# Output weights brought in and split during the last attention pass, half of the first output tile computed there, and that pass unrolled in another order

## The reference, cut to what matters

```python
s = jnp.einsum('bqhnd,bkhnd->bnhqk', q, k) * (1.0 / math.sqrt(HEAD_DIM))   # n = 0, 1: two score maps
a = jax.nn.softmax(s, axis=-1)
a = a[:, 0] - lam * a[:, 1]
attn = jnp.einsum('bhqk,bkhv->bqhv', a, v)
...
mix = jnp.concatenate([pool, attn], axis=-1) @ w_out
x = x + gate1 * mix
h2 = rms_norm(x, norm2_g) * (1 + scale2) + shift2
aff = softmax(h2 @ w_router)
```

## Time and profile before

| what | value |
|---|---|
| median of 3 runs | 3293.43 us (3290.72 to 3294.23) |
| the profiled execution | 3294.67 us, of it 3293.0 us from the first to the last instruction |
| PE busy with products | 3132.0 us (95%) |
| PE busy with weight loads | 2953.8 us (90%) |
| DVE, ACT, POOL busy | 2258.2 us (69%), 1640.5 us (50%), 650.2 us (20%) |
| mean granted clock of PE | 0.981 |

### The profile page before, as it was taken

One profiled execution on the slowest core, in us unless ns is written; L12 is line 12 of the kernel. 1 busy time (PEld: TensorE's weight loads), 2 busy tenths in 40 slices (PEclk: granted clock), 3 DMA queues, 4 the chain that ended last, 5 costly groups with the idle time before them and its releaser, 6 DMA issues. The chain is left out here.

```text
span 3293.0 us, 69969 instructions
## 1 busy us (share of the span) xinstructions
PE 3132.0 (95%) x23550; PEld 2953.8 (90%) x23550; DVE 2258.2 (69%) x3849; ACT 1640.5 (50%) x3632; POOL 650.2 (20%) x862
## 2 busy tenths in 40 slices
PE   6999999999999999998979985999999999999998
PEld 4988989989989999997768874999999999999998
DVE  4888888878878888878874447555555555555553
ACT  4556666666656656665652114443443444444442
POOL 2532333333333333331000001000100000000001
PEclk8999999999999999999989997999999999999999
DMA  8654344444344344433326544666666666665663
GB/s 286 239 196 131 120 146 125 127 130 137 118 134 141 121 128 153 127 101 102 112 96 245 192 156 141 192 188 189 199 187 188 190 188 186 189 192 180 191 187 97
DMA packets 373848, 530.69 MB, mean 161 GB/s; under 512 B 29658, under 2 KB 321754, under 8 KB 358490
## 3 DMA queue, kind: packets, MB, share of 16 engines
q1 hardware_dynamic: 363996, 494.52, 46.2%
q0 software_dynamic: 9728, 34.61, 4.6%
HBM read 439.10 MB, written 89.16 MB: 160 GB/s over the span
## 5 line engine op out<-in xcount | busy, mean ns | idle before, releaser
L2610 PE MATMUL ps_gu<-xT,e_w 128*128 128x272 f32 x6144 | 786.2, 290 | 2.1 <-DVE xT L2794 2.1
L2610 PEld LDWEIGHTS ps_gu<-xT,e_w 128*128 128x128 f32 x6144 | 776.8, 188 | 2.5 <-issue 2.3
L2783 DVE TENSOR_TENSOR e_w<-e_raw,e_w 128x2048 fp32r<-128x2048 f32 x190 | 435.3, 2291 | 413.6 <-ACT e_w L2683 413.6
L1082 ACT ACTIVATE e<-ps_s,negm 128x1024 f32<-128x1024 f32 (+2 forms) x416 | 474.3, 1146 | 257.2 <-DVE negm L1472 200.5
L1457 DVE TENSOR_REDUCE mx<-ps_s 128x1 f32<-128x1024 f32 (+3 forms) x428 | 524.4, 1233 | 78.5 <-PE ps_s L745 77.8
L745 PE MATMUL ps_s<-kT,qT 128*128 128x512 f32 (+1 forms) x1920 | 472.7, 385 | 12.6 <-ACT e L1082 11.6
L745 PEld LDWEIGHTS ps_s<-kT,qT 128*128 128x128 f32 x1920 | 341.9, 190 | 88.7 <-ACT e L1082 31.1
L2629 PE MATMUL ps_gu<-hid,e_w 128*128 128x272 f32 x3072 | 412.2, 291 | 0.0
L819 PE MATMUL ps_m<-w,hT 128*128 128x384 f32 x2040 | 391.7, 340 | 3.9 <-DVE o L1524 3.9
L2629 PEld LDWEIGHTS ps_gu<-hid,e_w 128*128 128x128 f32 x3072 | 392.2, 188 | 0.0
L787 PE MATMUL ps_m<-v,aT 128*128 128x128 f32 x2816 | 370.8, 277 | 1.2 <-ACT aT L1068 1.2
(11 more groups left out here) (333 smaller groups left out, 3472.8 us busy)
## 6 DMA issues: line engine op xcount, KB each, us to landing
hT<-hT_d SPq DMA_DIRECT2D x85, 1024.0 KB, 5.3
e_raw<-w_gate SPq DMA_DIRECT2D x64, 1024.0 KB, 5.0
e_raw<-w_up SPq DMA_DIRECT2D x64, 1024.0 KB, 5.0
e_raw<-w_down SPq DMA_DIRECT2D x64, 1024.0 KB, 5.6
tab<-tabs_d SPq DMA_DIRECT2D x85, 256.0 KB, 2.7
hT_d<-hT SPq DMA_DIRECT2D x17, 1024.0 KB, 3.9
cat_o<-cat_d SPq DMA_DIRECT2D x17, 1024.0 KB, 6.0
w_lent<-w_ada SPq DMA_DIRECT2D x16, 1024.0 KB, 5.5
```

The source lines that it names most:

```text
L1082: nc.scalar.activation(out, src, ACT.Exp, bias=negm[:, s.par, c:c + 1], scale=HD ** -0.5, accum_out=acc).then_inc(exp_done.sem, 1)
L2610: mm = nc.tensor.matmul(ps_gu[:, 2 * (s % 2) + f, 0:SLOTS], w_view(s, a)[:, k, f * P:f * P + P], xT[:, b, k, :], start=(k == 0 and a + b = ...
L2783: nc.vector.tensor_tensor(w[:, s % RING, 1, :], raw[:, s % RAW, :], w[:, s % RING, 0, :].bitcast(F32), ALU.subtract).then_inc(w_lo, 1)
```

## The change

Seven edits. (1) Pass 6 is written out, 17 steps without a loop. (2) SP loads w_out's eight blocks in step 2 of pass 6, into SBUF of that stage that pass 6 no longer uses. In steps 4 to 11 ACT rounds one block at the end of its step, and POOL subtracts it in four pieces of 128x256. (3) At the end of step 15 SP loads `cat` of tile 0, and `last_body` of PE computes k = 0 to 3 of tile 0's products between its steps. (4) `stage_output` keeps w_out and that `cat` where they are, starts tile 0 at k = 4, and loads and splits no w_out. (5) The modulation's result moves from `ps_m` to the fifth bank of `ps_s`: it waits for the maxima of c0 instead of for evacuate, `weighted` 0 no longer waits for its copy, and in that bank exp c0 g2 waits for it and scores c1 g2 for its copy. (6) PE, ACT and DVE get another order in late steps. (7) `last_body` begins with `turn` 4 of p. The late step then reads:

```diff
+SPLIT_FROM, LOWS, KS_AHEAD = 4, 4, 4
 def run_steps(eng, h, body):
+    if h == H:
+        for i in range(NT):
+            body(Slot(h, i))
+        return
...
+        def split_of(s):
+            return s.i - SPLIT_FROM if s.h == H and SPLIT_FROM <= s.i < SPLIT_FROM + KD else None
+        def mod_at(s):
+            return ps_s[:, KEYS + P:KEYS + P + 64] if late(s) else ps_m[:, 0:64]
...
+            def load_out(s):
+                qkv_ready.wait(sp, s)
+                s_ready.wait(sp, s)
+                for k in range(KD):
+                    sp.dma_start(wo_raw[k], io["w_out"][0, k * P:k * P + P, :]).then_inc(side_in, 16)
+            def load_first_rows(s):
+                first = Slot(H, 1)
+                sp.wait_ge(side_in, 16 + 16 * KD)
+                cat_saved[first.par].wait(sp, first, 16)
+                cat_saved[1 - first.par].wait(sp, first)
...
+                pv_part.wait(sp, s)
+                sp.dma_start(g.cat_first.bitcast(F32).rearrange("p k l n -> p (k l n)"),
+                             g.cat[0].rearrange("p k l c -> p (k l c)")).then_inc(side_in, 16)
             def body(s):
+                if s.h == H and s.i == 2:
+                    load_out(s)
+                if s.h == H and s.i == NS - 1:
+                    load_first_rows(s)
...
+                    if n == 2 and c == 1:
+                        mod2_done.wait(pe, s, 1)
...
-                    mod2_done.wait(pe, s, 1 if late(s) and (s.j is not None or s.i < NS) else 0)
+                    mod2_done.wait(pe, s)
...
-                o_done.wait(pe, s, 0 if late(s) else 1)
+                if late(s):
+                    mx_part.wait(pe, s, maxima_of(s))
+                else:
+                    o_done.wait(pe, s, 1)
...
+            def first_rows(k):
+                for a, b in ((0, 0), (0, 1), (1, 0)):
+                    for half in range(2):
+                        nc.tensor.matmul(ps_s[:, 512 * half:512 * half + 512], g.cat_first[:, k, a, :],
+                                         g.wo[b][k][:, 512 * half:512 * half + 512], start=(k == 0 and a + b == 0), stop=False)
             def last_body(s):
                 p = previous(s)
+                turn(p, 4)
                 weighted(p, 3)
                 weighted(p, 4)
+                pe.wait_ge(side_in, 16 + 16 * KD + 16)
+                pe.wait_ge(side_hi, 1 + KD)
+                pe.wait_ge(side_lo, 1 + LOWS * KD)
+                exp_done.wait(pe, s)
+                first_rows(0)
                 turn(s, 0)
+                first_rows(1)
                 weighted(s, 0)
                 turn_out(p)
+                first_rows(2)
                 o_lo.wait(pe, s)
+                first_rows(3)
                 turn_out(s)
...
 # ScalarE, GpSimd
+                    if n == 2 and c == 0:
+                        ada2_done.wait(act, s, 1)
...
+                if split_of(s) is not None:
+                    k = split_of(s)
+                    act.wait_ge(side_in, 16 + 16 * KD)
+                    nc.scalar.copy(g.wo[0][k], wo_raw[k]).then_inc(side_hi, 1)
...
+                if split_of(s) is not None:
+                    k = split_of(s)
+                    pool.wait_ge(side_hi, 1 + k + 1)
+                    for n in range(LOWS):
+                        sl = slice(D // LOWS * n, D // LOWS * (n + 1))
+                        nc.gpsimd.tensor_tensor(g.wo[1][k][:, sl], wo_raw[k][:, sl],
+                                                g.wo[0][k][:, sl].bitcast(F32), ALU.subtract).then_inc(side_lo, 1)
...
 # stage_output
-            for k in range(KD):
-                sp.dma_start(w_raw[:, k, :], io["w_out"][0, k * P:k * P + P, :]).then_inc(wraw_in[k], 16)
-                if k == 0:
-                    load_cat(0, 0)
+            sp.sem_inc(cat_in[0], 16)
+            load_cat(1, 1)
             load_row(0, 0, gate_in)
             load_x(0, 0, 0)
-            load_cat(1, 1)
...
-                for k in range(KD):
-                    if isinstance(t, int) and t == 0:
-                        pe.wait_ge(whi, k + 1)
-                        pe.wait_ge(wlo, k + 1)
+                for k in range(KS_AHEAD if isinstance(t, int) and t == 0 else 0, KD):
```

More of the change, by code:

```diff
@@ L698, in _, with scores @@
         def _(pe):
-            def scores(s, c):
+            def scores(s, c, some=slice(None)):
                 head = s.h - 1
-                if c == 0:
+                if c == 0 and not some.start:
                     if s.front == "sample":
@@ L712, in scores @@
                             v_copied.wait(pe, s)
-                for n, (lo, hi) in enumerate(groups_of(s)):
+                for n, (lo, hi) in list(enumerate(groups_of(s)))[some]:
+                    if n == 2 and c == 1:
+                        mod2_done.wait(pe, s, 1)
                     if c == 1 and s.front == "sample":
@@ L975, in late_body @@
                 p = previous(s)
-                scores(s, 0)
+                scores(s, 0, slice(0, 1))
+                if late(p):
+                    turn(p, 4)
+                scores(s, 0, slice(1, None))
                 if late(p):
@@ L987, in late_body @@
                 weighted(s, 1)
-                turn(s, 3)
+                weighted(s, 2)
                 if late(p):
@@ L1705, in late_body @@
                 mix(s, 2)
-                mix(s, 3)
                 for n in range(len(groups_of(s))):
@@ L1713, in late_body @@
                     normal_out(p)
+                mix(s, 3)
                 mix(s, 4)
@@ L1860, in sem, with fill_to @@
             return sems[-1]
-        w_raw = sb("wo_raw", [P, KD, D])
-        w = sb("wo", [P, 2, KD, D], F32R)
-        rows = sb("mod_rows", [P, 2, 3, D])
-        g2 = sb("g2", [P, D])
-        cat = sb("cat_o", [P, 2, KD, 2, P], F32R)
+        def fill_to(name, address):
+            start = aligned(nc.sbuf_base)
+            assert start <= address
+            if start < address:
+                sb(name, [P, (address - start) // 4])
+            assert aligned(nc.sbuf_base) == address
+        fill_to("wo_in_kT", g.home["kT"] + 4 * 2 * KEYS)
         xt = sb("x_o", [P, 2, D])
         x1 = sb("x1", [P, 2, D])
+        g2 = sb("g2", [P, D])
+        fill_to("free_kT", g.home["v"])
+        sb("cat_first", [P, KD * 2 * P])
         h2 = sb("h2", [P, 2, D])
+        fill_to("wo_in_raw", g.home["w"])
+        rows = sb("mod_rows", [P, 2, 3, D])
+        fill_to("wo_in_w", g.home["hT"] + 4 * 4 * KD * P)
+        cat = [g.cat_first, sb("cat_second", [P, KD, 2, P], F32R)[:]]
         h2T = sb("h2T", [P, KD, P])
@@ L1883, in stage_output @@
         ps_l = ctx.enter_context(nc.psum_tensor("ps_l", [P, 512], F32))
-        wraw_in, whi, wlo = [sem(f"wo_in{k}") for k in range(KD)], sem("wo_hi"), sem("wo_lo")
         gate_in, rows_in, rows_made = sem("gate_in"), sem("rows_in"), sem("rows_made")
@@ L2053, in body @@
                     sl = slice(512 * half, 512 * half + 512)
-                    nc.vector.tensor_tensor(x1[:, par, sl], ps_y[:, par, half, :], rows[:, prompt, 0, sl],
+                    nc.vector.tensor_tensor(x1[:, par, sl], y_of(t, par)[:, half, :], rows[:, prompt, 0, sl],
                                             ALU.mult).then_inc(gated, 1)
@@ L2078, in _ @@
         def _(act):
-            for k in range(KD):
-                act.wait_ge(wraw_in[k], 16)
-                nc.scalar.copy(w[:, 0, k, :], w_raw[:, k, :]).then_inc(whi, 1)
             def exponentials(t):
```

78 lines of the change are left out of this document (54 added, 24 removed).

## The result

| | before | changed |
|---|---|---|
| median of the runs (range), us | 3293.83 (3290.72 to 3297.70), 4 runs | 3273.16 (3270.16 to 3274.29), 4 runs |
| profiled execution, its span, us | 3294.67, 3293.0 | 3274.29, 3272.6 |
| instructions | 69,969 | 69,178 |

The ratio is 0.9938 (95% interval 0.9923 to 0.9953): the changed kernel is 20.7 us faster, by the interval some 15 to 25. Run again beside others it took 3275.52 (3271.41 to 3276.23, 5 runs), ratio 0.9935 (0.9922 to 0.9949).

A forecast was written before the change was run, and what follows sets the result against it. It took PE and DVE as nearly full in late steps, transfers as binding the output stage's front, and PE after it. Terms of -15.9, +0.5, +1.6, +0.7, +0.8 and -14.1 sum to -26.4: 3293.4 becomes 3267.0 us, range 3257 to 3282.

The forecast's parts named there:

- Term 2: POOL's subtractions in pass 6: 32 pieces delay DVE by 0.2 us in each of 8 steps, +1.6 us.
- Term 3: Pass 6's end: step 16 costs +0.7 us and the products added to last_body +0.8 us.
- Term 4: Output stage's front: with w_out already loaded, rows land earlier and tile 2 starts at 1739.5 instead of 1753.59, -14.1 us.
- Term 1: Pass 6's late steps: the new order and unrolling cut the period from 13.28 to 12.15 us, -15.9 us over 14 steps.
- DVE's floor: Late step of pass 6: DVE's own sequence without its waits for scores, 11.95 us, the least for any order.
- Rival A: Late steps: lateness goes round in the new order, period stays at 13.0 us, total 3279 us; chance 0.17.
- Rival C: Late steps: POOL's pieces block DVE's mixes, +10 to +22 us, total 3277 to 3289; chance 0.07.
- Rival D: Unrolled pass 6 starves for instructions: a gap in each of 12 steps, +40 us, total 3307; chance 0.04.
- Step 1: Step 1 of pass 6: moving mix 3 behind `negm` puts up to 0.7 us on the path, +0.5 us.
- Step 16: Pass 6's end: evacuate of tiles 14 and 15 each comes 0.35 us later behind turn 4, +0.7 us.
- last_body: Pass 6's end: of the added blocks of tile 0's products, the second delays the prompt's weighted, +0.8 us.
- Rival B: Output stage's front: tile 0's chain is late by itself, gain only 6 us, total 3275 us; chance 0.10.

The follow-up runs named there:

- experiment 1: The kernel before with pass 6 written out and nothing else: 3296.15 us, ratio 1.0003 to the kernel before.
- experiment 2: The changed kernel with the old order of late steps and the modulation back in `ps_m`: 3286.64 us, ratio 0.9971 to the kernel before.
- experiment 7: The changed kernel with the low halves of w_out subtracted by DVE, one 128x1024 in each of eight steps, none by POOL: 3279.50 us, ratio 0.9951.
- experiment 6: The changed kernel without products of tile 0 computed ahead in `last_body`; w_out still loaded early: 3276.66 us, ratio 0.9946.
- experiment 5: The changed kernel with, in step 1 alone, `turn` 0 and 1 ahead of the modulation and mix 3 ahead of c1's maxima: 3272.26 us, ratio 0.9930.
- experiment 8: The changed kernel with the edits of experiments 3, 4 and 5 together: 3265.68 us, ratio 0.9912 to the kernel before.
- experiment 10: The kernel of experiment 8 run again, side by side with the changed kernel: 3264.81 us, ratio 0.9906 to the kernel before.
- experiment 3: The changed kernel with, in step 16 alone, turn 4 and weighted 3 ahead of the prompt's scores: 3270.26 us, ratio 0.9927.
- experiment 9: The changed kernel itself run again, side by side with the kernel of experiment 10: 3275.52 us, ratio 0.9935 to the kernel before.
- experiment 4: The changed kernel with `cat` of tile 2 issued ahead of tile 0's stores instead of behind its store of h: 3267.71 us, ratio 0.9914.

## Why the prediction was right, and where it was off

The time, 3273.16, is in the range of 3257 to 3282 and 6.2 us above the 3267.0 forecast, near the upper end of the forecast's own range (3259 to 3274). The forecast's likeliest case is what happened, 20.7 gained instead of 26.4. Part of how near it came is luck: Term 2 was put 1.6 too high and so made up for some of what Terms 3 and 4 lacked, and 2.0 of the 20.4 us between the two traces lie ahead of all that was edited.

**Term 1 holds.** 12.17 against the 12.15 taken, 13.16 outside the loop before. That it is the order and the bank, and not the unrolling or the early load, experiments 1 and 2 show: with the pass written out alone, and with the early load, POOL's pieces and the half tile on top of that, the period stays at 13.16. It is 0.22 above the 11.95 that the prediction called DVE's floor, and experiment 7 shows that DVE bounds it. The wait that is left stands where the layout put it, ahead of the second maximum of c1, but also ahead of that of c0, where it looked for none. Rival A (the order closes on itself) falls with the period.

**Term 2 was an overestimate: 0 instead of +1.6.** Steps with pieces (1579.50 to 1591.66, 12.16) and the mean of all 14 (12.17) are the same; `on` takes 0.28. The pieces lie where the layout put them, 2.7 us ahead of N to N + 0.1. Rival C falls: 32 pieces of 0.73 beside DVE's maxima cost nothing that a period shows. The Trainium skill (page "SBUF — State Buffer", section "Who interferes with whom") names two cases in which a DVE instruction and GpSimd lock each other out, two SBUF inputs on DVE against a GpSimd read, and DVE's two-port modes; maxima have one input, in PSUM, and by that rule too they go free: the trace agrees, with 12.16 beside 12.17. Where the two did meet on a mix, it was POOL that took longer: in experiment 2 a piece begun 0.28 us before mix 3's end takes 0.88 instead of 0.73 and the two mixes keep their 1.40, and the power takes 0.99 beside mixes, 0.56 in the passes before. No run laid whole pieces on the mixes, so what rival C would have cost stays unshown.

**Rival D falls.** Experiment 1 is the whole of it, ratio 1.0003.

**Step 1 was mis-sized**, +1.7 instead of +0.5. The prediction followed mix 3 and missed a wait: with its result in the bank of the scores, the modulation waits for the maxima of c0, and in step 1 nothing stands in front of it. PE stood still for 2.6 us ahead of it, then ran it at the low clock (1.93 us, 1.10 in the kernel before), with scores of c1, `turn` 0 and 1 queued behind it. That gap did not bring the clock down: it was 0.50 from 1494 to 1496 already, when PE was busy, and in experiment 6 the same modulation ran in 1.10 behind a wait of 2.24. "The modulation's earlier release costs nothing" was right for the late steps and was not asked for step 1. Experiment 5 gives 2.1 us back against the changed kernel's trace, 1.6 in the mean of all traces.

**Step 16 was mis-sized**, +3.6 instead of +0.7, the furthest from its forecast in proportion (in microseconds Term 4's miss is larger). Its order by itself is not the miss: experiment 7 ran the same two pieces at full clock in 6.47 + 8.91 = 15.38, against 5.93 + 9.05 = 14.98 before, +0.4. The other 3.2 are the clock, which Term 3 did not price. The prompt's scores stand ahead of `weighted` 3 and 4 now and need exp c1 g2, which is ready only at 1680.5. PE is busy 0.61 of the 2 us before 1680, the granted clock is 0.50 from 1682 to 1684, and 16 products take 3.34 instead of 2.00. The second piece (10.50) lost its clock without the new order as well, in experiments 1 and 2 (10.42), and lost or kept it with one and the same code in experiments 8 and 10, so the part of the miss that stands there (1.45) is not the order's doing. The first piece had the low clock in four of six traces of the new order and in none of three of the old, where PE's gap ahead of the prompt's scores is 1.50 us and not 1.94. So the new order may have its part in that loss; it is not shown.

**last_body was right**: +0.6 against +0.8, and by its reason: the prompt's `weighted` starts 3.32 us behind evacuate 15 (1698.70) instead of 2.44, 0.9 later. That experiment 6, without the products, has 7.37 for this piece instead of 7.23 does not speak against it, since the granted clock was 0.50 there and 1.00 in the changed kernel; the old code at the low clock takes 7.02 (experiment 1).

**Term 4 was right in its mechanism and too large**, -11.9 and then +2.6 lost in tile 2, 9.3 instead of 14.1. Two steps of it were off. `make_rows` came 13.3 behind the start and not 11: the third row's issue was stuck 3.53 us again (10.74 before), and landed later than bytes over rate would have it. And from the issue of `cat` of tile 2 to tile 2's start it took the 6.4 us that the forecast took too (6.53), but PE was done sooner than that, stood still for 2.56 us until 1730.04, and ran tile 2 at the clock of 0.50: the step "whatever moves the start of tile 2 moves everything behind it by as much" left out what the clock is when tile 2 starts. The same two products took 1.22 behind waits of 2.3 to 2.7 us in experiments 2, 3, 5 and 9 too and 0.73 behind one of 1.04 in experiment 6, but also 1.22 behind one of 0.67 in experiment 7. Experiment 4 takes the wait away and wins 5.5 us, 3.0 of the start and 2.6 of the clock, as the two traces have it. The forecast of 22.5 for tile 2 was met only by that kernel (21.7). Rival B, the front gains less, is what happened in part: 9.3 is between its 6 and the forecast's 14.1. Of the missing 4.8, 2.2 are the late third row, one of B's causes, though `make_rows` stayed under the 15 us that were to be its sign; 2.6 are the clock behind the wait, which B did not have.

**Left open.** Why the same code in step 16 held its clock in experiments 5 and 7 and lost it in the changed kernel, and why one and the same kernel did both (experiments 8 and 10), was not settled. Nor was an earlier place for the router's load, behind which the third row's issue was stuck, tried.

## What to carry to other kernels

When an order is tightened, lay out not only the steady step but the first and the last one: there the instruction that moved up meets a producer that is still late, and everything behind it on its engine waits as well. On PE such a gap of 2 us or so can be paid for twice, once as a wait and once in low clock behind it (it was not each time here), so put work there that is ready. Before a microsecond or two in one piece of a trace is credited to an edit, look whether the same code takes the same time in other traces. And when a front is bound by one queue, after taking bytes out of it look at what stands in the queue ahead of the next load: one load moved ahead of a few stores brought 5.5 us, over half as much as the 4 MB moved out of the stage.

## What the runs showed of the hardware

- The same step 16 took 6.47 or 8.05 us, and the next piece 8.91 or 10.4 to 10.5, in executions that differed in edits elsewhere only, and the next piece 8.91 or 10.49 in two executions of one kernel (experiments 8 and 10). The difference is the granted clock, 1.00 or 0.50 (2.4 or 1.2 GHz), which fell behind a gap of PE in one and held behind the same gap in another. Small gains from edits are hidden or doubled by this: experiment 1 won 1.7 us in its steps and showed none at the end.
- Writing out the 12 looped steps took away 0.12 us a step in the mean of 14 and cost nothing that the time shows, with 78 packets of instructions fetched instead of 67.
- Where POOL worked beside DVE's mixes, POOL's instructions grew and DVE's did not: a 128x256 subtraction 0.88 instead of 0.73 us, the mixes 0.74 each in both orders. Beside DVE's maxima of PSUM neither grew.
- A DMA issue on SP can be stuck by what is queued: the third row's took 3.53 us here and 10.74 with the weights in the queue, where the others of the changed kernel's front take 0.34 to 0.85 up to that of `cat` of tile 2.
